# A two-layer encoder trunk on one core: state space inputs turned by TensorE, gated stage mixed block by block, constant products in TensorE's waits

## The reference

```python
shift, scale, gate = adaln(c_act, ada_w[layer, k], ada_b[layer, k])
h = x * (1.0 + scale) + shift
y = ...                                    # the mixer of the layer, or the MLP
x = layer_norm(ALPHA * x + (1.0 + gate) * y, ln_g[layer, k], ln_b[layer, k])
```

```python
# 128 groups of 16 channels, 64 complex states each, both directions
s = associative_scan(a * s_prev + B u);  y = d * u + Re(C s), summed over directions
z = jax.nn.gelu(y) @ w_glu;  a, g = split(z);  y = a * sigmoid(g)
```

## Time and profile before

| | |
|---|---|
| median of the runs | 2853.85 us |
| profiled execution | 2854.89 us |
| its span, first to last instruction | 2853.09 us |
| TensorE busy | 2626.1 us (92%) |
| VectorE busy | 1885.3 us (66%) |
| ScalarE busy | 1103.2 us (39%) |
| GpSimd busy | 122.1 us (4%) |
| moved by DMA | 636.98 MB, mean 223 GB/s |

### The profile page before, as it was taken

How to read it: one execution, slowest core, us unless ns; L and a number is a source line. 1 busy time by engine, 2 the same in 40 slices (tenths; PEclk the granted TensorE clock), 3 DMA queues, 4 the chain that set the end, 5 groups by cost and what they waited for, 6 DMA issues and landing times.

```text
span 2853.1 us, 43744 instructions
## 1 busy us (share of the span) xinstructions
PE 2626.1 (92%) x17484; PEld 2113.2 (74%) x17484; DVE 1885.3 (66%) x1930; ACT 1103.2 (39%) x881; POOL 122.1 (4%) x174
## 2 busy tenths in 40 slices
PE   6989999967788999999999967899889999999997
PEld 2348888823477888888888851688778888888886
DVE  6876666678456776777777748666676666555554
ACT  4453333354433333344444421134333333444442
POOL 1011000000000100000000031000020000000000
PEclk9999999987889999999999978999999999999998
DMA  8888878722342887887878849478657777555551
GB/s 243 340 314 292 284 255 285 253 67 82 119 148 97 290 283 264 288 279 266 286 265 282 292 144 222 161 240 282 230 163 238 235 233 238 175 191 177 191 191 44
DMA packets 251405, 636.98 MB, mean 223 GB/s; under 512 B 39683, under 2 KB 40837, under 8 KB 246693
## 3 DMA queue, kind: packets, MB, share of 16 engines
q1 hardware_dynamic: 234788, 579.73, 61.1%
q0 software_dynamic: 10176, 35.13, 4.2%
q10 hardware_dynamic: 6336, 20.65, 1.9%
HBM read 613.57 MB, written 19.79 MB: 222 GB/s over the span
## 4 chain that ended last, share of the span: by engine, by line
PE 82%; DVE 12%; ACT 2%; DMA 1%; issue 1%; ACTq 1%; SPq 0%; DVEq 0%
PE PS L271 47%; PE PS L275 23%; PE PS L224 3%; DVE Pb L1829 2%; DVE acc L1824 1%; PE PS L928 1%; PE PS L728 1%; DMA araw<-in_ada_w 1%; DVE wlo L261 1%; PE PS L188 1%; ACT Pb L1004 1%; PE PS L749 1%; ACTq L428 1%; PE PS L454 1%; PE PS L661 1%
## 5 line engine op out<-in xcount | busy, mean ns | idle before, releaser
L271 PE MATMUL PS<-H,whi 128*128 128x512 f32 x5888 | 1864.6, 398 | 50.6 <-DVE wlo L261 26.0
L261 DVE TENSOR_TENSOR wlo<-raw,whi 128x2048 fp32r<-128x2048 f32 x368 | 844.1, 2294 | 705.0 <-ACT whi L257 703.9
L275 PEld LDWEIGHTS PS<-H,wlo 128*128 128x128 f32 x5888 | 1113.5, 189 | 262.8
L257 ACT ACTIVATE whi<-raw 128x2048 fp32r<-128x2048 f32 x368 | 705.4, 1917 | 1229.5 <-PE PS L271 1208.0
L275 PE MATMUL PS<-H,wlo 128*128 128x256 f32 x5888 | 1162.5, 279 | 0.0
L271 PEld LDWEIGHTS PS<-H,whi 128*128 128x128 f32 x5888 | 904.4, 190 | 55.7 <-DVE wlo L261 32.1
L180 DVE SCALAR_TENSOR_TENSOR acc<-araw,cact,acc 128x1024 f32<-128x1024 f32 x240 | 307.6, 1282 | 1.3 <-DMA araw<-in_ada_w 0.8
L1004 ACT ACTIVATE Pb<-PS 128x1024 f32 (+5 forms) x117 | 118.4, 1036 | 136.9 <-PE PS L661 52.2
L1004 ACT ACTIVATE H<-Pb 128x512 fp32r (+3 forms) x138 | 90.5, 657 | 36.9 <-DVE Pb L1465 23.2
L1513 DVE TENSOR_TENSOR H<-Pb,H 128x512 fp32r<-128x512 f32 x128 | 87.6, 685 | 0.0
L1942 POOL TENSOR_SCALAR X<-X,small 128x256 f32<-128x256 f32 x64 | 64.8, 1031 | 484.0 <-DVE Pb L1465 475.4
(11 more groups left out here) (269 smaller groups left out, 1331.6 us busy)
## 6 DMA issues: line engine op xcount, KB each, us to landing
raw<-in_mlp_w SPq DMA_DIRECT2D x256, 1024.0 KB, 5.9
araw<-in_ada_w SPq DMA_DIRECT2D x274, 512.0 KB, 4.5
raw<-in_mix_w_in SPq DMA_DIRECT2D x64, 1024.0 KB, 7.6
raw<-in_s_w_glu SPq DMA_DIRECT2D x32, 1024.0 KB, 7.2
acc<-in_ada_w SPq DMA_DIRECT2D x40, 512.0 KB, 8.2
raw<-in_ada_w POOLq DMA_DIRECT2D x32, 512.0 KB, 4.0
raw<-in_mix_w_out SPq DMA_DIRECT2D x16, 1024.0 KB, 5.2
vmat<-Pb ACTq DMA_DIRECT2D x8, 1024.0 KB, 7.4
```

Source lines behind the costliest of these rows:

```text
L257: nc.scalar.activation(whi[:, s % 2, :], raw[:, s, :], ACT.Copy).then_inc(S("hi_done"), 1)
L261: nc.vector.tensor_tensor(wlo[:, s % 2, :], raw[:, s, :], whi[:, s % 2, :].bitcast(F), ALU.subtract).then_inc(S("lo_done"), 1)
L271: return nc.tensor.matmul(PS[:, b, :], w, H2[:, :, k, :], start=first, stop=last, skip_group_check=True)
L275: return nc.tensor.matmul(PS[:, b, 0:T], w, H2[:, 0, k, :], start=False, stop=last, skip_group_check=True)
```

## The change

The 64 DMAs of spread go. In their place TensorE multiplies HS by SEL, rows of the identity that SP loads into acc (8 DMAs): for each half 16 products, on four row groups of 32, into four PSUM banks. ScalarE copies half 0 and half of half 1 to UT, VectorE the rest. Of each group of state products ScalarE then copies one component (c = 0) and VectorE the other; VectorE forms YT in four pieces between. The first four shift slices are asked for before POOL scales X, and wait for GATE2's sum instead of its finish. In the gated stage each block is mixed (glu_mix) in VectorE's list: blocks 0 and 1 ahead of splits in later blocks, block 2 before the last addition, block 3 after it; the sum of SCALE3 moves between the two sums of the norm. Last, products of constants (idle_products, result never read) are put at TensorE's waits: in both head norms, in one attention step and after the squares of the first, third and fourth layer norms.

```diff
-    def spread(q, half, share, landed="u_ready"):
-    ...
+    SEL = acc[:, 512:1024].rearrange("p (j m) -> p j m", j=4)
+    UTV = UT.rearrange("p (k a) n -> p a k n", a=4)
+    def state_part(n, c):
+        b = 4 - 4 * (n % 2) + 2 * c
+        return (SV[:, 1:64, c, 16 * n:16 * n + 16].rearrange("p n (t g) -> p g t n", g=2),
+                PS[:, b:b + 2, :].rearrange("p g (t n) -> p g t n", t=8)[:, :, :, 0:63])
+    def idle_products(n, b):
+        for _ in range(n):
+            nc.tensor.matmul(PS[:, b, 0:T], ones[:, 0:P], ones[:], start=True, stop=True)
     def rms_pe(pe, n):
+        if n == 2:
+            idle_products(8, 1)
         pe.wait_ge(S("rms_sq"), n)
...
+        idle_products(8 if n == 1 else 5, 7)
         pe.wait_ge(S("rms_inv"), n)
...
+        if n == 2:
+            idle_products(30, 7)
@@ sync
-                    for half in range(2):
-                        spread(sp, half, 0)
+                    sp.wait_ge(S(f"{SCALE2.name}_freed"), 1)
+                    for a_ in range(4):
+                        for g in range(2):
+                            load(SEL[32 * a_ + 16 * g:32 * a_ + 16 * g + 16],
+                                 a["ident"][64 * g:64 * g + 64].rearrange("(j c) m -> c j m", j=4), "ld_sel")
@@ layer_norm_pe, between the sums and at the end
+                elif k == 2:
+                    ada_sum(pe, SCALE3, 0)
...
+                else:
+                    idle_products(26 if k == 3 else 19, 7)
@@ attention_pe, after the transposes of step n
+                    if n == 9:
+                        idle_products(14, 7)
@@ s5_pe
-                pe.wait_ge(S(f"{GATE2.name}_freed"), 1)
+                pe.wait_ge(S("ld_sel"), 128)
+                for half in range(2):
+                    pe.wait_ge(S("hs_ready"), half + 1)
+                    if half:
+                        pe.wait_ge(S(f"{GATE2.name}_freed"), 1)
+                    for j in range(4):
+                        for a_ in range(4):
+                            rows_ = slice(32 * a_, 32 * a_ + 32)
+                            last = nc.tensor.matmul(PS[:, 4 - 4 * half + a_, :], SEL[rows_, j, :],
+                                                    HS[rows_, 8 * half:8 * half + 8, j, :],
+                                                    start=(j == 0), stop=(j == 3))
+                    last.then_inc(S("u_mm"), 1)
@@ before the glu stage's norm
-                    run_sum(plan_glu[1], 0, 1)
@@ s5_act
-                for half in range(2):
-                    spread(act, half, 1)
+                act.wait_ge(S("u_mm"), 1)
+                run(UTV[:, :, 0:8], PS[:, 4:8, :].rearrange("p a (k n) -> p a k n", k=8), sem="u_evac")
+                act.wait_ge(S("u_mm"), 2)
+                run(UTV[:, 0:2, 8:16], PS[:, 0:2, :].rearrange("p a (k n) -> p a k n", k=8), sem="u_evac")
                 for n in range(8):
                     act.wait_ge(S("mat_used"), n + 1)
-                    for c in range(2):
-                    ...
+                    run(*state_part(n, 0), sem="sv_evac")
@@ vector
+            def glu_mix(blk):
+                if blk == 0:
+                    v.wait_ge(S("x_scaled"), 3)
+                v.wait_ge(S("sig_done"), blk + 1)
+                value = Pb[:, 16 + 4 * blk:20 + 4 * blk, :]
+                link(tt(value, value, Pb[:, 32 + 4 * blk:36 + 4 * blk, :], ALU.mult))
+                for kt in range(4 * blk, 4 * blk + 4):
+                    xv = X[:, kt].rearrange("p (n j) -> p j n", j=4)
+                    stt(xv, Pb[:, 16 + kt].rearrange("p (j n) -> p j n", j=4), G1[:, 2, kt:kt + 1], xv,
+                        ALU.mult, ALU.add).then_inc(S("x_mixed"), 1)
@@ split_lows
                         for sl in range(4):
+                            if s is plan_glu[1] and sl == 0 and i >= 2:
+                                glu_mix(i - 2)
@@ vector, state space stage
-                    link(tt(YT, UT, Dsk[:].unsqueeze(2).broadcast_to([P, 64, 64]), ALU.mult))
+                    v.wait_ge(S("u_mm"), 2)
+                    link(nc.vector.tensor_copy(UTV[:, 2:4, 8:16], PS[:, 2:4, :].rearrange("p a (k n) -> p a k n", k=8)))
+                    v.sem_inc(S("u_copied"), 1)
...
+                    v.wait_ge(S("u_evac"), 2)
+                    for n in range(8):
+                        v.wait_ge(S("mat_used"), n + 1)
+                        nc.vector.tensor_copy(*state_part(n, 1)).then_inc(S("sv_copied"), 1)
+                        if n % 2:
+                            ts_ = slice(8 * n - 8, 8 * n + 8)
+                            link(tt(YT[:, ts_], UT[:, ts_], Dsk[:, ts_].unsqueeze(2).broadcast_to([P, 16, 64]),
+                                    ALU.mult))
@@ vector, end of the gated stage
                     prev = split_lows(plan_glu, early=2)
+                    glu_mix(2)
                     add_block(*prev, 1)
-                    ada_finish(v, link, SCALE3, 0)
-                    v.wait_ge(S("sig_done"), 4)
-                    v.wait_ge(S("x_scaled"), 3)
-                    link(tt(PF[:, 4096:8192], PF[:, 4096:8192], PF[:, 8192:12288], ALU.mult))
-                    ...
-                    layer_norm(2, plan_mlp[1][0][0], between=lambda: modulation(3, 2))
+                    glu_mix(3)
+                    def scale_three():
+                        ada_finish(v, link, SCALE3, 0)
+                        modulation(3, 2)
+                    layer_norm(2, plan_mlp[1][0][0], between=scale_three)
@@ gpsimd
-            for half in range(2):
-                spread(pool, half, 2, "u_soft")
-            scale_x(2)
             for c in range(32):
+                if c == 4:
+                    pool.wait_ge(S("hs_ready"), 2)
+                    scale_x(2)
                 if c < 4:
                     pool.wait_ge(S("ada_used"), SCALE3.base + PRIME_ADA)
-                    pool.wait_ge(S(f"{GATE2.name}_freed"), 1)
+                    pool.wait_ge(S(f"{GATE2.name}_summed"), 1)
```

More of the change, by code:

```diff
@@ L420, in trunk @@
     LN_BANK = (1, 3)
-    def spread(q, half, share, landed="u_ready"):
-        q.wait_ge(S("hs_ready"), half + 1)
-        ks = slice(8 * half, 8 * half + 8)
-        for i in range(share, 32, 3):
-            g, j, a_ = i // 16, i // 4 % 4, i % 4
-            q.dma_start(UT[64 * g + 16 * j:64 * g + 16 * j + 16].rearrange("p (k a) n -> p a k n", a=4)[:, a_, ks],
-                        HS[32 * a_ + 16 * g:32 * a_ + 16 * g + 16, ks, j, :]).then_inc(S(f"{landed}{half}"), 16)
+    SEL = acc[:, 512:1024].rearrange("p (j m) -> p j m", j=4)
[4 more added lines that the diff above has]
+                PS[:, b:b + 2, :].rearrange("p g (t n) -> p g t n", t=8)[:, :, :, 0:63])
     def shift_part(pe, c):
@@ L879, in matrices @@
                     return raw[:, n % 4, :]
-                pe.wait_ge(S(f"{GATE2.name}_freed"), 1)
+                pe.wait_ge(S("ld_sel"), 128)
[10 more added lines that the diff above has]
+                    last.then_inc(S("u_mm"), 1)
                 for n in range(8):
-                    if n in (0, 4):
-                        pe.wait_ge(S(f"u_ready{n // 4}"), 352)
-                        pe.wait_ge(S(f"u_soft{n // 4}"), 160)
+                    if n < 2:
+                        pe.wait_ge(S("u_evac"), n + 1)
+                    if n == 1:
+                        pe.wait_ge(S("u_copied"), 1)
                     mats = matrices(n).rearrange("p (x m) -> p x m", x=16)
@@ L888, in s5_pe @@
                         pe.wait_ge(S("sv_evac"), n - 1)
+                        pe.wait_ge(S("sv_copied"), n - 1)
                     for t in range(8):
@@ L899, in s5_pe @@
                 pe.wait_ge(S("sv_evac"), 8)
+                pe.wait_ge(S("sv_copied"), 8)
                 pe.wait_ge(S("win_ready"), 3)
@@ L1224, in s5_act @@
             def s5_act():
-                for half in range(2):
-                    spread(act, half, 1)
+                act.wait_ge(S("u_mm"), 1)
+                run(UTV[:, :, 0:8], PS[:, 4:8, :].rearrange("p a (k n) -> p a k n", k=8), sem="u_evac")
+                act.wait_ge(S("u_mm"), 2)
+                run(UTV[:, 0:2, 8:16], PS[:, 0:2, :].rearrange("p a (k n) -> p a k n", k=8), sem="u_evac")
                 for n in range(8):
                     act.wait_ge(S("mat_used"), n + 1)
-                    for c in range(2):
-                        ins = run(SV[:, 1:64, c, 16 * n:16 * n + 16].rearrange("p n (t g) -> p g t n", g=2),
-                                  PS[:, 4 * (n % 2) + 2 * c:4 * (n % 2) + 2 * c + 2, :].rearrange(
-                                      "p g (t n) -> p g t n", t=8)[:, :, :, 0:63])
-                    ins.then_inc(S("sv_evac"), 1)
+                    run(*state_part(n, 0), sem="sv_evac")
                 act.wait_ge(S("shift_used"), 32)
@@ L1530, in body @@
                                     ada_mac(v, u, i, k0, 1, 0, sl // 2, first and k0 == 0)
-                    for i in range(2):
-                        body(i, i, i == 0, prev, True)
```

(24 more changed lines are left out.)

3 lines of the change are left out of this document (2 added, 1 removed).

## The result

The changed kernel takes 2829.18 us (median; 2826.22 to 2834.69) where the kernel before, run beside it, takes 2854.03 (2853.52 to 2855.88): a ratio of 0.9909, 95% interval 0.9894 to 0.9924. 24.9 us are gained; 24.7 were forecast, inside the range.

The account below looks back on a forecast made before the run. Streamed products on TensorE bound the kernel, so gains come from seams: -8.5 - 8.3 - 1.5 - 2.4 - 4.5 + 1.5 - 1.0 = -24.7 from 2854.9, less 1.04, gives 2829 us; range 2813 to 2843.

Parts of the forecast that it names:

- The turn: State inputs turned on TensorE: first half 6.7 us, to 1680.4, second 4.4, to 1684.8, if four row groups work at once.
- The gaps between groups: State products: unnamed waits for code stay, period 3.6 us a group; scan at 1716.6, 8.5 us gained (3 to 20).
- The rival without waits for code: State products: code is not awaited, period 2.09 us, scan at 1704.5, kernel 2817 us; chance 0.20.
- The copies out: State products: ScalarE 1.76 us a group, VectorE between 1.23 and 1.76 plus YT pieces, both cheaper than TensorE.
- the first rival: State products: code is not awaited, period 2.09 us a group, kernel 2817 us; chance 0.20.
- The gated stage: Blocks mixed early: splits delayed +1.2 us (0 to 3), third norm's centring earlier by 10.5.
- The term for the moved sum: Third norm: SCALE3's sum between its two sums makes centring to reciprocal 2.2 us longer, 12.60 against 10.44.
- Second head norm: Idle products of 8 and 5 in its waits: at most -5.1 us, taken as -3.0.
- the projection's start: Thirty idle products, 13.2 us in a wait of 14.00, speed the output projection's slow start: -1.5 us.
- thirty products at 1.2 GHz: Rival before the output projection: clock stays down, 26.4 us in a wait of 14.00, kernel 2846 us; chance 0.10.
- First MLP: 19 idle products start TensorE faster, but its slab wait grows from 1.74 to 4.7 us: +1.5 (0 to 2.5).
- Last norm: 26 idle products before the final transposes, then ScalarE's copies bind: -1.0 us (0 to -1.5).

Follow-up runs that it names:

- the first profile: Profiled execution of the unaltered changed kernel, the longest of its runs: 2834.69 us (span 2832.9).
- both edits together: Changed kernel with SCALE3's sum moved into the wait for the third norm's last mix and no idle products behind the first norm: 2825.97 us, ratio 0.9898.
- the second profile: Another profile of the same unaltered changed kernel: 2830.38 us (span 2828.6).

## Why the prediction came out right, and where it did not

**The turn: right.** The half was priced at 4.4 us at full clock and 6.7 for the first. Both took 9.39 against 11.1: a round of four passes takes 0.85 us at the low level and 0.43 at the high one, the four starting within 0.05 us of each other. The Trainium skill ("TensorE: Matmul & The Clock Gate", "Part 3: Packing small matmuls — row/col tiling") gives 3.07 times the rate for four row groups of 32 rows and 512 columns; here four passes take the time of one (0.85 us at the low level, the step from pass to pass in one row group with the loops exchanged), so 4 times; where the two differ the measured rate counts, and the order of the loops decides how many of them meet.

**The gaps between groups: right in size, the cause now shown.** The eight groups take 30.5 us, a period of 3.8 us against 3.6; the scan comes 7.9 us earlier against 8.5. The rival without waits for code (0.20) is refuted by the gaps after 127, 128 or 255 passes, each ended by a packet of code. The sequence of the Trainium skill ("Runtime: NRT & Kernel Launch", "Instruction fetch mechanics") fits in its blocks of 256 instructions, 128 passes with their weight loads; its "mostly hidden" doesn't: a block gives TensorE 2.09 us of work and costs 0.6 to 3.0 us of waiting on top.

**The copies out: the size was wrong, without a price.** A state copy on VectorE was put between 1.23 and 1.76 us. It took 1.90 beside ScalarE's 1.92, and 2.3 to 2.4 in all later groups, and ScalarE's copies rose from 1.76 to 2.3 and 2.4 too. Two copies and a YT piece (1.25) make 6.0 us in two groups of 7.6: covered by the code waits. Without those, by my estimate from these copies, VectorE would have been the bound at 3.0 us a group, and the first rival's 2817 would not have come either.

**The gated stage: the step was right, its follow-up was not.** Centring came 8.3 us earlier where 1.2 - 10.5 = -9.3 was forecast; 1.1 us of the difference is the last tiles, which ran at 1.2 GHz, 3.06 us against 1.99. The term for the moved sum, +2.2, was read off the norm that already had it. But the two norms compared there differ in the clock as well. TensorE's timeline of the kernel before shows the squares of its second and of its third norm, and that of the turn alone the squares of a third norm that no edit touches:

```profile
1657.42 8.84 PE L749 MATMUL PS<-Pb,ones 128*128 128x256 f32 x32
2071.41 7.17 PE L749 MATMUL PS<-Pb,ones 128*128 128x256 f32 x32 [2.41 <-ACT Pb L1004]
```
```profile
2060.29 8.86 PE L761 MATMUL PS<-Pb,ones 128*128 128x256 f32 x32 [2.40 <-ACT Pb L1034]
```

1.7 of the 2.2 us are squares that ran partly at the 1.2 GHz level (PEclk 0.81 from 1657.4 to 1666.3, against 1.00 from 2071.4 to 2078.6). Without any edit there the third norm's stretch takes 10.44 us in the kernel before, 11.77 and 11.76 with the turn or the constants alone. The mixes alone have the slow squares too (8.84); against those two kernels the moved sum costs 0.9 us, so their +2.2 bears out the figure and not the cause that was given for it. In the change the clock did more: the last tiles, the sum (6.82 us against 3.63) and part of the squares ran at the low level for 13.7 us. Neither the wait before the last tiles nor the sum's place is the sole cause: filled, the stretch is 14.3 us, with the sum elsewhere 11.7 to 12.7, with nothing altered but what ran long before it 12.7 or 16.7, and 16.5 in the change itself. What decides between these stays open. The mistake was to take the cost of a move from one place in one profile and to give it no bounds, though the clock there is not the edit's own.

**Second head norm: too careful.** I took -3.0 of -5.1 since 12-row products might drop the clock. The sums held it in all profiles with the constants, 3.62 us instead of 5.31; the wide ones took 3.71 instead of 7.00 in the first profile and 5.05 in the second. So the norm gave 5.0 and 3.6 us. The thirty products behind it take 14.90 us instead of 13.2 and end after the wait of 14.00: the projection's start gives 0.9 and 0.5 us instead of 1.5. The case "thirty products at 1.2 GHz" did not come.

**First MLP: right in kind.** The wait for the third slab appears (2.56 us, behind another of 0.99, where 4.7 was forecast), and the products after it run at the low level, 0.79 us for a pass, in both profiles. From reciprocal to first relu, behind the constants, this cost 2.1 and 0.8 us, against +1.5 (0 to 2.5). The +5.1 of the first profile has two parts more: 1.4 in the first norm, ahead of these constants (squares of 8.86 us against 7.17), and 1.6 in the rest of the MLP, unchanged code.

**Last norm: undersized.** 3.2 us against 1.0: 1.5 from the final transposes, as argued, and 1.7 from the last norm's squares, for which nothing was edited. They ran that much faster in both profiles and in three of the seven later kernels built on the change (loops exchanged, constants in the wait, both edits together), and as before in the other four. The timelines of the kernel before and of the first profile show the same two values as above:

```profile
2820.87 8.86 PE L749 MATMUL PS<-Pb,ones 128*128 128x256 f32 x32 [2.48 <-ACT Pb L1004]
```
```profile
2803.91 7.17 PE L763 MATMUL PS<-Pb,ones 128*128 128x256 f32 x32 [2.48 <-ACT Pb L1035]
```

PEclk is 0.81 from 2820.8 to 2829.8 in the one and 1.00 from 2803.9 to 2811.1 in the other. So this is the clock again, in code that no edit touches, and 1.7 of the 3.2 us are luck.

**Start: luck.** Unchanged code up to the attention's step 9 came 1.1 and 2.9 us earlier, in other kernels up to 3.8 earlier or 1.0 later. So the -24.5 of the second profile holds 2.9 that no step of the sum claims, beside the 1.7 of the last norm, and against them 3.9 lost in the third.

## What to carry to other kernels

Idle gaps that nothing on the page explains, at equal counts of instructions rather than at waits, were waits for straight-line code here: relieving the engines around them gains only what was above them, and half as much code again cost 22 us in a stage of 46. Look whether a packet of the instruction queue ends just before each gap does. Put products on different row groups next to each other, the row group in the inner loop; here the order, not the tile, gave the overlap, and with it the clock rose. A term that depends on TensorE's clock needs both levels in its range, even where a like place of the same kernel shows one; and before two like places are compared, the same instructions in both (here the squares) should be read for the level they ran at.

## What the hardware showed that I had not expected

- Straight-line products on TensorE, 128 passes and 128 weight loads to a stretch of work of 2.09 us: a wait of 1.74 to 2.02 us before each, every 3.8 to 4.1 us, in a profile of the kernel without the first norm's constants. With half as much code again, 1536 passes against 1024, 12 packets of instructions against 7. Each of these packets has 16384 bytes, and each such wait, 82 in 13 profiles, ended 1.2 to 1.6 us after one had ended.
- Passes on 32 rows and 512 columns, two row groups at once and no pause, left the clock at 0.50 for the 32 us that they lasted; with four row groups at once it rose after 4.6 us. While one-column products of 128 rows ran without a pause it fell from 1.00 to 0.50 in one kernel and stayed at 1.00 in another.
- Strided copies of 1008 elements out of PSUM take 1.90 us on VectorE and 1.76 to 1.92 on ScalarE at first, and 2.3 to 2.4 on both in the later groups, where both copy at once while TensorE's products run. Which of the two makes them slower was not tested.
- The same 32 products of a layer norm's squares, in unchanged code, take 7.17 us in one place or profile and 8.84 to 8.86 in another, at a granted clock of 1.00 or of 0.81.
